# Moving the causal mask of two softmax attentions to VectorE and the scaling of their probabilities to GpSimd

## The reference

```python
sc = einsum('bhqd,bhkd->bhqk', qi, k) * scale          # fox adds ci[:, None] - c[None, :]
sc = where(kpos[None, :] <= qpos[:, None], sc, NEG)
p = softmax(sc, axis=-1)
o = einsum('bhqk,bhkd->bhqd', p, v)
```

## Time and profile before

| | |
|---|---|
| median of 3 runs | 903.08 us (902.74 to 903.2) |
| the profiled execution | 903.16 us, of which its span is 901.3 us |
| TensorE matmuls, busy | 895.0 us (99%) |
| GpSimd, busy | 497.6 us (55%) |
| VectorE, busy | 389.5 us (43%) |
| ScalarE, busy | 342.6 us (38%) |
| granted clock of TensorE | 1.00 over the whole span |
| fox attention | about 147 to 209 us |
| mla attention | about 391 to 455 us |

### The profile page before, as it was taken

How to read it: one execution, slowest core, us unless ns; L and a number is a source line. 1 busy time by engine, 2 the same in 40 slices (tenths; PEclk the granted TensorE clock), 3 DMA queues, 4 the chain that set the end, 5 groups by cost and what they waited for, 6 DMA issues and landing times.

```text
span 901.3 us, 12927 instructions
## 1 busy us (share of the span) xinstructions
PE 895.0 (99%) x4528; PEld 737.6 (82%) x4528; DVE 389.5 (43%) x684; ACT 342.6 (38%) x693; POOL 497.6 (55%) x515
## 2 busy tenths in 40 slices
PE   8999999999999999999999999999999999999998
PEld 7889888777779888876779988888888888888887
DVE  2743494667743653765657611111111122223672
ACT  4333403556726221565648522222222223223421
POOL 7988795311565877823246454444444455555453
PEclk9999999999999999999999999999999999999999
DMA  6434532103222332321012342222332322223213
GB/s 218 123 133 132 146 99 94 42 30 117 72 70 71 117 95 93 103 84 47 6 57 99 104 136 93 93 93 93 97 106 99 117 94 93 93 93 103 73 59 117
DMA packets 28412, 85.73 MB, mean 95 GB/s; under 512 B 5064, under 2 KB 8016, under 8 KB 28240
## 3 DMA queue, kind: packets, MB, share of 16 engines
q1 hardware_dynamic: 24528, 78.65, 26.3%
q10 hardware_dynamic: 3840, 6.48, 2.6%
HBM read 80.93 MB, written 2.10 MB: 92 GB/s over the span
## 4 chain that ended last, share of the span: by engine, by line
PE 98%; POOL 1%; DMA 0%; DVE 0%; ACT 0%; issue 0%; SPq 0%; ACTq 0%
PE bank L502 28%; PE bank L504 28%; PE bank L503 28%; PE bank L559 5%; PE bank L747 2%; PE bank L1081 2%; PE bank L844 1%; POOL w_lo L455 1%; PE bank L808 1%; PE bank L810 1%; PE bank L809 1%; PE bank L836 1%; PE bank L873 1%; DMA raw<-in_weights 0%; PE bank L726 0%; PE bank L614 0%
## 5 line engine op out<-in xcount | busy, mean ns | idle before, releaser
L455 POOL TENSOR_TENSOR w_lo<-raw,w_hi 128x256 fp32r<-128x256 f32 (+1 forms) x420 | 411.0, 1007 | 205.9 <-ACT w_hi L1327 200.1
L502 PE MATMUL bank<-aT_hi,w_hi 128*128 128x512 f32 (+1 forms) x584 | 225.8, 387 | 0.0
L504 PE MATMUL bank<-aT_hi,w_lo 128*128 128x512 f32 (+1 forms) x584 | 222.4, 381 | 0.0
L503 PE MATMUL bank<-aT_lo,w_hi 128*128 128x512 f32 (+1 forms) x584 | 222.2, 381 | 0.0
L502 PE MATMUL bank<-w_hi,aT_hi 128*128 128x512 f32 (+3 forms) x576 | 218.5, 379 | 0.5 <-POOL w_lo L455 0.4
L504 PE MATMUL bank<-w_hi,aT_lo 128*128 128x512 f32 (+3 forms) x576 | 213.2, 370 | 0.0
L503 PE MATMUL bank<-w_lo,aT_hi 128*128 128x512 f32 (+3 forms) x576 | 212.8, 370 | 0.0
L447 POOL TENSOR_SCALAR w_hi<-raw 128x1024 fp32r<-128x1024 f32 x70 | 76.2, 1088 | 178.5 <-PE bank L504 141.1
L1327 ACT ACTIVATE w_hi<-raw 128x1024 fp32r<-128x1024 f32 x70 | 74.2, 1060 | 232.2 <-PE bank L504 216.7
L504 PEld LDWEIGHTS bank<-aT_hi,w_lo 128*128 128x128 f32 x584 | 109.8, 188 | 21.2
L503 PEld LDWEIGHTS bank<-aT_lo,w_hi 128*128 128x128 f32 x584 | 110.0, 188 | 19.8 <-issue 0.2
(11 more groups left out here) (235 smaller groups left out, 920.2 us busy)
## 6 DMA issues: line engine op xcount, KB each, us to landing
raw<-in_weights SPq DMA_DIRECT2D x141, 512.0 KB, 3.3
q_swapped<-q_parts ACTq DMA_DIRECT2D x2, 1024.0 KB, 12.0
x<-in_x ACTq DMA_DIRECT2D x4, 512.0 KB, 5.4
y_out<-x SPq DMA_DIRECT2D x7, 256.0 KB, 4.1
x<-in_x SPq DMA_DIRECT2D x3, 512.0 KB, 7.4
g_post<-in_gains ACTq DMA_DIRECT2D x3, 512.0 KB, 3.3
x<-in_x SPq DMA_DIRECT2D x2, 256.0 KB, 3.7
raw<-in_weights SPq DMA_DIRECT2D x2, 256.0 KB, 4.6
```

Source lines behind the costliest of these rows:

```text
L455: lo = nc.gpsimd.tensor_tensor(w_lo[:, s, at], raw[:, r, at], w_hi[:, s, at].bitcast(F32), ALU.subtract)
L502: mm(out, st_hi, mv_hi, start=start, stop=False)
L503: mm(out, st_hi, mv_lo, start=False, stop=False)
L504: return mm(out, st_lo, mv_hi, start=False, stop=stop)
```

## The change

The bf16 mask matmul is taken out of `scores`; the last score matmul now closes the group and counts `scored`. VectorE adds `mask_le`, now in float32, to the last 128 columns of the bank in place, waits for its own addition (`masked`), and then takes the maximum. VectorE no longer scales the probabilities: its reciprocal counts `sums_turned`, and GpSimd, which waits for that, does the scaling and counts `normed`. GpSimd's program for the three chunks beside each attention is written out around these 32 scalings: `whole_hi` (1024 columns) behind the scaling of one step, `lo_quarter` (256 columns) behind the scalings of the next four. In mla the last chunk begins at step 29, so that its last two quarters follow step 31. The pieces of out2a in and behind the tail of mla come in another order: row 1 of group 0 first, then row 0 of group 1.

```diff
--- before.py
+++ after.py
@@ -230,7 +230,7 @@
         c_head = sb("c_head", [P, FOX_H], F32R)
         ident = sb("ident", [P, P])
         ident_b = sb("ident_b", [P, P], BF16)
-        mask_le = sb("mask_le", [P, P], BF16)
+        mask_le = sb("mask_le", [P, P])
         mask_lt = sb("mask_lt", [P, P], BF16)
         neg_tri = sb("neg_tri", [P, P])
         neg_one = sb("neg_one", [P, P])
@@ -331,7 +331,8 @@
         sines = sem("sines")
         angles = sem("angles")
 
-        scored, maxed, exped, normed = sem("scored"), sem("maxed"), sem("exped"), sem("normed")
+        scored, masked, maxed = sem("scored"), sem("masked"), sem("maxed")
+        exped, sums_turned, normed = sem("exped"), sem("sums_turned"), sem("normed")
         turned, pt_made, pv_done, pv_drained = sem("turned"), sem("pt_made"), sem("pv_done"), sem("pv_drained")
 
         z_full, z_abs, z_exp, z_ln, sp_made = sem("z_full"), sem("z_abs"), sem("z_exp"), sem("z_ln"), sem("sp_made")
@@ -474,7 +475,56 @@
                 for c in range(a, b):
                     split(c, c % SLOTS, shared, skipped=skipped, own=own, parts=parts)
 
-            splits(0, SHARED, False, parts=4)
+            def scale_probs(base, heads, between):
+
+                for m in range(heads * T):
+                    n, kw = base + m, (m % T + 1) * P
+                    pool.wait_ge(sums_turned, n + 1)
+                    nc.gpsimd.tensor_scalar(P_buf[:, n % 4, 0:kw], P_buf[:, n % 4, 0:kw], erec[:, n % 8:n % 8 + 1],
+                                            None, ALU.mult).then_inc(normed, 1)
+                    between(m)
+
+            def whole_hi(c):
+
+                s, r = c % SLOTS, c % RAW
+                pool.wait_ge(raw_in[r], (c - r) * (16 // RAW) + 16)
+                pool.wait_ge(w_used, c - SLOTS + 1)
+                nc.gpsimd.tensor_scalar(w_hi[:, s, :], raw[:, r, :], 1.0, 1.0, ALU.mult, ALU.mult).then_inc(hi_made, 1)
+
+            def lo_quarter(c, n):
+
+                s, r = c % SLOTS, c % RAW
+                if n == 0:
+                    pool.wait_ge(hi_made, c + 1)
+                at = slice(n * CW // 4, (n + 1) * CW // 4)
+                lo = nc.gpsimd.tensor_tensor(w_lo[:, s, at], raw[:, r, at], w_hi[:, s, at].bitcast(F32), ALU.subtract)
+                if n == 3:
+                    lo.then_inc(w_split, 1)
+
+            def chunk_between(c, first, m):
+
+                if m == first:
+                    whole_hi(c)
+                elif first < m <= first + 4:
+                    lo_quarter(c, m - first - 1)
+
+            def fox_between(m):
+                chunk_between(CH["out1"], 9, m)
+                chunk_between(CH["out1"] + 1, 17, m)
+                chunk_between(CH["out1"] + 2, 25, m)
+
+            def mla_between(m):
+                chunk_between(CH["out2a"], 16, m)
+                chunk_between(CH["out2a"] + 1, 21, m)
+                chunk_between(CH["out2a"] + 2, 29, m)
+                for n in range(2 if m == MLA_H * T - 1 else 0):
+                    lo_quarter(CH["out2a"] + 2, n + 2)
+
+            splits(0, CH["out1"], False, parts=4)
+            scale_probs(0, FOX_H, fox_between)
+            splits(CH["out1"] + 3, CH["out2a"], False, parts=4)
+            scale_probs(FOX_H * T, MLA_H, mla_between)
+            splits(CH["out2a"] + 3, SHARED, False, parts=4)
             splits(SHARED, CH["ffn"] + SLOTS, True, parts=4)
             splits(CH["ffn"] + SLOTS, CH["pgate"], True)
             splits(CH["pgate"], GATE_HI[0], False, skipped=CH["pgate"] - SHARED)
@@ -722,8 +772,7 @@
                         first(m)
                     out = bank[n % 3]
                     kw = (qb + 1) * P
-                    score_(out[:, 0:kw], i, qb, kw)
-                    mm(out[:, qb * P:kw], ident_b[:, :], mask_le[:, :], start=False, stop=True).then_inc(scored, 1)
+                    score_(out[:, 0:kw], i, qb, kw).then_inc(scored, 1)
 
                 def turn_probs(m):
                     qb = m % T
@@ -807,8 +856,8 @@
                 c_at = 0 if qb < 2 else S // 2
                 mm(out, q_parts[:, i, at], k_parts[:, i, 0:kw], start=True, stop=False)
                 mm(out, q_swapped[:, i, at], k_parts[:, i, 0:kw], start=False, stop=False)
-                mm(out, c_head[0:HD + FOX_H, i:i + 1].broadcast_to([HD + FOX_H, P]),
-                   c_parts[0:HD + FOX_H, c_at:c_at + kw], start=False, stop=False)
+                return mm(out, c_head[0:HD + FOX_H, i:i + 1].broadcast_to([HD + FOX_H, P]),
+                          c_parts[0:HD + FOX_H, c_at:c_at + kw], start=False, stop=True)
 
             pe.wait_ge(k_lo, FOX_H)
             pe.wait_ge(q_swapped_in, 32)
@@ -1074,20 +1123,22 @@
             def out2a_tail(j):
                 if j == 0:
                     left_ready(3)
-                for g, k in (((0, 0), (0, 1)), ((0, 2),), ((1, 0), (1, 1)))[j]:
-                    out2a_block(0, g, k)
+                if j == 2:
+                    pe.wait_ge(exped, (FOX_H + MLA_H) * T)
+                for t, g, k in (((0, 0, 0), (0, 0, 1)), ((0, 0, 2),), ((1, 0, 0), (1, 0, 1)))[j]:
+                    out2a_block(t, g, k)
 
             def mla_score(out, i, qb, kw):
-                mm(out, q2T[0:QK2, i, qb * P:(qb + 1) * P], k2T[0:QK2, i, 0:kw], start=True, stop=False)
+                return mm(out, q2T[0:QK2, i, qb * P:(qb + 1) * P], k2T[0:QK2, i, 0:kw], start=True, stop=True)
 
             softmax_attention(FOX_H * T, MLA_H, mla_score, v2, out2c_piece,
                               first=lambda m: pe.wait_ge(drained["act"], tiles["q2T", 2][3][1]),
                               tail=out2a_tail, tail_first=True)
             pe.wait_ge(exped, (FOX_H + MLA_H) * T)
             pe.wait_ge(pt_made, (FOX_H + MLA_H) * T)
+            out2a_block(1, 0, 2)
             for k in range(3):
-                out2a_block(1, 0, k)
-            out2a_block(0, 1, 2)
+                out2a_block(0, 1, k)
             left_ready(1)
             pe.wait_ge(pv_drained, (FOX_H + MLA_H) // 2)
             out2a_block(0, 0, 3)
@@ -2003,15 +2054,17 @@
                         n = base + m
                         kw = (m % T + 1) * P
                         dve.wait_ge(scored, n + 1)
+                        own_keys = bank[n % 3][:, kw - P:kw]
+                        V.tensor_tensor(own_keys, own_keys, mask_le[:, :], ALU.add).then_inc(masked, 1)
+                        dve.wait_ge(masked, n + 1)
                         V.tensor_reduce(negmax[:, n % 8:n % 8 + 1], bank[n % 3][:, 0:kw], AX_X, ALU.max, negate=True)\
                             .then_inc(maxed, 1)
                     if m > 0:
                         n = base + m - 1
-                        kw = ((m - 1) % T + 1) * P
                         dve.wait_ge(exped, n + 1)
-                        own(V.reciprocal(erec[:, n % 8:n % 8 + 1], esum[:, n % 8:n % 8 + 1]))
-                        V.tensor_scalar(P_buf[:, n % 4, 0:kw], P_buf[:, n % 4, 0:kw], erec[:, n % 8:n % 8 + 1],
-                                        None, ALU.mult).then_inc(normed, 1)
+                        if n >= 8:
+                            dve.wait_ge(normed, n - 7)
+                        V.reciprocal(erec[:, n % 8:n % 8 + 1], esum[:, n % 8:n % 8 + 1]).then_inc(sums_turned, 1)
 
                     if m % (2 * T) == T + 1 and m > 2 * T:
                         pair_out(m // (2 * T) - 1)
```

## The result

The changed kernel takes 909.46 us (median of 5 runs, 908.65 to 910.07), against 903.2 for the kernel before in the same comparison (902.74 to 903.67): ratio 1.0067, interval 1.0056 to 1.0078. It is 6.3 us slower. The forecast was 899.6 and its range ended at 903.2; of the cases, it is the slow rival. The profiled execution took 909.09, with a span of 907.2 at a granted clock of 1.00.

What follows compares the result with a forecast made beforehand. TensorE, busy 895.0 of 901.3 us, was taken as the bound. Slots 4.6, less stalls 0.5, 0.2 and 0.2 and 0.2 for single late steps, gave 3.5 us: median 899.6, range 898.3 to 903.2.

Steps and rivals of the forecast that it cites:

- the slow rival: Rival for both attentions: GpSimd's scaling by an SBUF scalar is much slower and comes late; 908 us, chance 0.12.
- The slots: TensorE in both attentions: 64 mask matmuls go and give back 4.6 us, bounds 3.5 to 4.7.
- The mask addition: VectorE, path from score to transpose: adding 128 x 128 out of the bank takes 0.34 us, bounds 0.25 and 0.6.
- The scaling on GpSimd: Path from score to transpose: 384 columns take 0.50 us on GpSimd, upper bound 1.2, against VectorE's 0.42.
- Steady steps cost nothing: Middle of both attentions: of 1.10 us slack before TensorE's transpose, 0.4 is left, so no stall there.
- Start of fox: First attention's start: the first scaling stands behind GpSimd's split of chunk sk1; stall 0.5 us, bounds 0.3 and 0.8.
- End of fox: First attention's end: the last quarter of chunk out1+2 stands behind step 29's scaling; stall 0.2 us, bounds 0 and 0.8.
- End of mla: Second attention's end: two quarters and all of out2a+3 follow the last scaling; 0.2 us, bounds 0 and 1.5.
- The reordering itself costs nothing: Tail of mla: the new order has the same blocks, and the exponentials it waits for are done; 0 us.
- What is won or lost there arrives at the end: Behind the two attentions: TensorE stays the chain, so their gains or losses reach the kernel's end in full.
- GpSimd is the path: Rival: scaling by an SBUF scalar is much slower, third block late at every head; 908 us at 1.5, chance 0.12.
- The shared port: Rival: VectorE and GpSimd wait for each other by up to 0.7 us; some 1.5 us more, 901.1, chance 0.16.

Runs made afterwards that it cites:

- e_nomask_pad: Kernel before without any causal mask in the two softmax attentions, plus 128 increments of an unused semaphore on TensorE; 898.96 us, ratio 0.9956.
- e_mask_only: Kernel before with the mask added by VectorE, which goes on scaling; mask matmul gone, GpSimd's program and the tail as before; 907.49 us, ratio 1.0048.
- e_pad: e_two_ops with 128 increments of an unused semaphore in TensorE's program, two behind the scores of each step; 900.63 us, ratio 0.9972.
- e_start: e_pad with the fourth quarter of chunk sk1 moved behind the first scaling at the start of fox; 900.17 us, ratio 0.997.
- e_two_ops: Changed kernel with GpSimd's scaling written as two operations, by the scalar in SBUF and then by 1.0; 902.17 us, ratio 0.9994.
- e_const: Changed kernel with GpSimd multiplying by constant 1.0 twice instead of by the reciprocal in SBUF, rows not normalised; 901.74 us, ratio 0.9991.
- e_forms: Changed kernel with four forms of GpSimd's scaling by head in turn: SBUF scalar or constant, one or two operations; one run, 905.67 us.

## Why the prediction was wrong, point by point

By medians: before 903.1, without masks and filled 898.96 (-4.1), with the addition, the two-operation scaling on GpSimd, the chunks in pieces and the new tail order, also filled, 900.63 (+1.7), with the one-operation scaling 907.82 (+7.2), without the filling 909.46 (+1.6). The last two steps are one edit each. The four add up to +6.4, as they must; the comparison at the top has +6.3, against its own median of before.

- **The slots: right.** Predicted 4.6, bounds 3.5 to 4.7; measured 1.94 + 2.05 = 4.0 by stages, 4.1 by medians. Between scores the slot is as read: from the fifth score on, fox gains 0.07 a step, and mla from the fourth on 0.06 (forecast 0.072 and 0.058). The six first steps were taken too high. In mla the three gain 0.3 together, where 0.4 was forecast. In fox the first four steps take 5.32 us in before and in e_nomask_pad alike: what the slots give there is lost at the first transpose, for VectorE's scaling of step 0, slow in before too (here), then ends last.

```profile
150.97 0.78 DVE L2013 TENSOR_SCALAR h<-h,erec 128x128 f32<-128x128 f32 x1
```

- **The mask addition: right.** 0.34 with the wait on itself, measured 0.298 and 0.33 from start to start (158.31, 158.64). "About as much" is roughly so: VectorE has 35.58 us in fox against 39.44. e_mask_only shows what it hung on.
- **The scaling on GpSimd: the step that failed.** It was taken as "0.50" for 384 columns, from the one-input rows, with 1.2 as the upper bound. It measured 1.27, above that bound. I noted that no row has a scalar in SBUF, and looked for the danger there. The real difference stood elsewhere in the same rows: those splits are written with `1.0, 1.0, ALU.mult, ALU.mult`, the new instruction with `None`. The rate was read from a row with the same name and another form. The term cost 7.2 us of the result, more than the whole loss. Why GpSimd needs longer for one operation than for two no run shows. The prediction also let its sum stand by the one-input rule of the Trainium skill ("GPSIMD Engine Reference", section 4.1, Engine selection), roughly line-rate; for the one-operation form that does not hold, 1.27 us against VectorE's 0.42, and the measurement decides.
- **"Steady steps cost nothing": right for 0.6 us but for a few late steps, wrong for 1.27.** From the fifth score of fox to the last, e_pad and e_start take 46.38 us, e_nomask_pad 46.53. In after GpSimd's fox work, 53.68 of 62 us, leaves no room: a scaling of 512, then a quarter, then the next, is longer than the 1.9 us step (1.57 + 0.70).
- **Start of fox: right.** Stall 0.5 predicted; from e_pad to e_start the first four steps fall from 5.57 to 5.05 us.
- **A path that the prediction doesn't have: ScalarE's copies.** ScalarE copies the transposed probabilities behind its next exponential, and TensorE may not transpose into that bank before. The addition makes the maximum, and with it the exponential and the copy, 0.3 us later. At one step in mla TensorE now waits for the copy (e_pad):

```profile
430.26 0.41 PE L610 MATMUL bank<-ident,h 128*128 128x128 f32 x2 [0.28 <-ACT PT L1381]
```

  That step takes 1.62 us instead of the 1.14 of e_nomask_pad: 0.48 lost, more than the 0.2 set aside for all single late steps.
- **End of fox: 0.5, not by the quarter.** 0.2 taken, bounds 0 and 0.8. From the last score to the end of fox e_pad takes 8.22 us, e_nomask_pad 7.73. The largest part, 0.3, is ahead of the transposes of step 29, and by the starts it is again the copy: in e_start ScalarE copies for step 27 from 199.51 to 200.10, and TensorE transposes at 200.24, while GpSimd's scaling of step 29 had ended at 199.55. e_start and e_nomask_pad have the same fox, 59.58, only because e_start gains 0.4 in the steps ahead of the last score, which it loses here (8.15).
- **End of mla: right.** 0.2 taken, bound 1.5. Behind the last score e_pad takes 8.93 us, e_nomask_pad 8.68. The rest of the 0.85 by which mla is longer is the late step above and 0.1 at the first transpose. All stalls were put at 1.1 and are 1.7 by medians, 1.4 by the two stages.
- **"The reordering itself costs nothing": right, and too little.** With the old order it would have cost 1.6 more.
- **Not in the prediction at all:** the gate stage. "What is won or lost there arrives at the end" held only if the instruction count stays; 1.6 us were lost there.
- **The rivals.** "GpSimd is the path" named the result and its size (908), with the chance of an unlikely case, 0.12. Its cause, the SBUF scalar, was wrong, and its size is near by luck: 908 was worked out at 1.5 us for 384 columns, and at 1.27 its rule gives 12 x 0.37 + 2 = 6.4 over the forecast, 906.0, where the filled kernel has 907.82. It counted waits at every fourth step and not the rows of GpSimd pieces behind each chunk. The shared port did not decide, though it shows. In e_pad a `mix_low` subtraction of two SBUF inputs took 0.82 instead of 0.68 just ahead of the late steps at the end of fox (197.8), and the addition in `mla_pair` 0.75 instead of 0.68 ahead of the one in mla (427.1). At the end of mla, in after, that addition took 0.68 (447.63) instead of the 1.35 in the earlier trace rows. The Trainium skill ("GPSIMD Engine Reference", section 3.1, Elementwise) has a body of up to two operations run at one rate, about a cycle an element. For two operations the runs agree roughly, (716 - 371) / 384 = 0.90 ns a column; for one operation they do not, 2.56, and the measurement decides.

With the fast form and the filling the same change gives 900.63 against the 899.6 forecast.

## What to carry over

Price an instruction from a row of the same form: engine, shapes and types are not enough, the number of its operations and their operands belong to it. Where there is no such row, the form that already runs in the kernel is the safe one to write. When a short producer is put between an engine's long pieces, add up the queue behind the longest piece, not only the single step's slack. When a path gets longer, follow every engine that hangs on it, also the one whose copy frees a buffer. When instructions go, look at the last loads of the program even if they lie hundreds of microseconds behind the edit: filling instructions that do nothing tell a shift of the program's own loading from a real cost.

## What the runs showed of the hardware

- GpSimd's TENSOR_SCALAR on float32 in SBUF: with one operation 2.56 ns a column (606 ns for 128, 1589 for 512), with two 0.90 (371 and 716). The scalar from SBUF instead of a constant: 74 to 76 ns more at all four sizes (e_two_ops against e_const), and with one operation as well (e_forms); with two operations e_forms has 75 more at 128 columns, but 15 less at 512.
- 128 semaphore increments in TensorE's stream cost it nothing that shows: fox 60.23 without and 60.17 with them, mla 62.78 both times.
- Packets of an instruction queue lie among the kernel's loads, 23 to 25 us apart toward its end. Where one of them started within 1 us of the last load's issue, from issue to split it was 4.9 to 6.1 us, else 4.1 to 4.3 (14 executions).
- VectorE's scaling of a tile in SBUF is held up by a GpSimd instruction that started first. In e_mask_only a scaling of 384 columns takes 0.42 us at 165.92, GpSimd idle, and 1.09 in GpSimd's pass over a raw chunk (1.08 and 1.07 at 174.40 and 189.48, in the same place):

```profile
159.14 1.05 POOL L447 TENSOR_SCALAR w_hi<-raw 128x1024 fp32r<-128x1024 f32 x1 [7.95 <-PE bank L504]
```
```profile
159.31 1.09 DVE L2015 TENSOR_SCALAR h<-h,erec 128x384 f32<-128x384 f32 x1
```

  VectorE's maximum out of a bank in e_pad, at 159.19, keeps its 0.29 beside a scaling on GpSimd (158.97 to 159.55). The Trainium skill ("SBUF — State Buffer", "Who interferes with whom") has a VectorE tensor_scalar able to take the port pair that both share, whole instruction by whole instruction, and the maximum not: the trace agrees.
